# Second block: softplus attention in head pairs, two units ahead, and 256-column products split into high and low parts

## The chip, the cores and the metric

The kernel runs on one core of a Trainium2 chip. The metric is the device time of one execution in microseconds (us). Three runs of the kernel before gave 3783.95, 3784.22 and 3786.22 us, so the median is 3784.22 us. One more execution was profiled. TensorE is called PE below, VectorE DVE, ScalarE ACT, GpSimd POOL and SyncE SP.

## What is computed

Two transformer trunks of depth 2 follow one another, on 256 tokens of width 1024. All arithmetic is in fp32. The first block (gated linear attention, latent attention, a convolution module and a convolutional feed-forward, with 256 context tokens beside the 256 tokens in its first layer) is not touched. The second block, with what matters of its reference:

```python
h = x
for i in range(2):
    u = rms_norm(h, g_mix_pre[i])
    y = stick_breaking_attention(...) if i == 0 else dilated_attention(...)
    h = h + rms_norm(y, g_mix_post[i])
    u = rms_norm(h, g_ffn_pre[i])
    f = square(relu(u @ w_ff_in[i])) @ w_ff_out[i]      # 1024 -> 4096 -> 1024
    h = h + rms_norm(f, g_ffn_post[i])
    gate = sigmoid(rms_norm(h, g_ple[i]) @ w_ple_gate[i])
    h = h + (p[i] @ w_ple[i]) * gate

# stick breaking, 16 heads of 64, per head:
z = q @ k.T / 8
log_fail = where(past, log_sigmoid(-z), 0)              # -softplus(z)
later = reverse_cumsum(log_fail) - log_fail
a = where(past, exp(log_sigmoid(z) + later), 0);  out = a @ v
# dilated: 3 groups (dilation 1, 4, 16) of 8 heads of 64, rotary on q and k,
# softmax per group, groups joined by their log-sum-exp; in the kernel one
# softmax over the 3 x 256 masked scores of a head and a query
```

The projections are `x @ w_in_sb` (1024 x 3072) and `x @ w_in_dil` (1024 x 4608).

## The kernel before

There is no scheduler. Each engine's program is written out by hand, as one function per engine, and a `Plan` object gives every PSUM tile (a result of up to 128 x 512 in one of eight banks) its place in PE's order, its bank and its semaphore count. The activations lie transposed: 8 tiles `k` of 128 features by 256 tokens.

**Weights.** SP streams them through `wring`, a ring of three slots of 1 MB. A chunk is 8 x 128 input rows by 256 output columns (or 16 x 128 rows by 128 columns for `w_ff_out`). The load of chunk n waits until PE is through with chunk n - 3 (line 621 and the lines around it).

**Products.** `cols` (L712) makes one output tile of 128 features by 256 tokens with 8 fp32 matmuls, the weights as the stationary operand. `rows_of` (L734) does the same for values, with the activations stationary and 256 columns of weights moving. `deep` (L752) sums over 32 input tiles for `w_ff_out`. The profile shows each fp32 matmul as two records, each with its own weight load.

In the second block there are 128 such products of 256 columns in `sqk` (queries and keys of layer 0), 64 in `sv` (its values), 192 in `dqk`, 96 in `dv` (layer 1), 256 in each layer's `ffin`, 256 in each `ffout` and 64 in each `pg` (the gate): 1632 in all. `b2out` (the attention's output projection) and `pw` are such products too.

**Split products.** The first block's layer 0 feed-forward already makes its products another way: ACT copies a weight tile as `fp32r` into `weights_hi`, POOL subtracts to give `weights_lo`, the activations are split likewise, and `parts` (L687) makes high x high, high x low and low x high, three `fp32r` matmuls per input tile, 512 columns each.

**Norms.** `sums` (L786) adds 8 tiles of squares. DVE's `rms` (L1787, L1780, L1782) and ACT's `root` give 1/rms. `pre` (L2197) then writes the operand, 8 multiplies of 128 x 256, and `post` (L2204, L2206) adds the normed result to the residual.

**Stick-breaking attention.** Head by head. PE: `logits` one head ahead (L1111, L1112), cumulative sums against a triangle of ones (L1124 to L1127), then for each second head the values of two heads (L1136 to L1138). ACT: scaled copy of z, Abs, Exp, Ln, and later Exp of the argument; a table load stands between Ln and Exp. DVE: `failures` (L2243, L2244), `argument` (L2253, L2255), the mask (L2260) and the output copy (L2266).

**Dilated attention.** 16 units (8 head slots x 2 query tiles; an even unit has 3 blocks of keys, an odd one 6). PE: scores (L1160) one unit ahead, transposes of the probabilities (L793), then the values (L1179), which wait for ACT's copy of the transposes. DVE: mask and maximum (L2289, L2293), the probabilities (L2310), the output copy (L2301).

**Feed-forward.** `ffin`: PE makes 32 tiles; ACT takes Relu out of PSUM (L1235) and DVE squares (L2318). `ffout` follows when all of `ff_h` is there.

Of the kernel before, what the change touches and what calls it, by code (L numbers as in the profile page):

```python
# [56 lines left out]
def shape_constants():  # L57
# [39 lines left out]
    strict = i[:, None] < i[None, :]  # L97
    add("stick", np.concatenate([strict, np.ones((P, P)), strict], 1), 1)
# [40 lines left out]
class Plan:  # L139
# [3 lines left out]
    def __init__(self):  # L143
# [6 lines left out]
        self.units, self.unit_at, self.split_after = [], {}, {}  # L150

# [24 lines left out]
    def gemm(self, name, chunks, split=lambda i: False, after=lambda: None):  # L176
# [4 lines left out]
        for i, (loads, ends) in enumerate(chunks):  # L181
# [22 lines left out]
def build(nc, a, consts, late_consts, masks, const_at, out):  # L204
# [68 lines left out]
    HF, _ = area(s_at, ("ff_h", [P, FT2, SEQ]))  # L273
# [3 lines left out]
    PD, PDT, _ = area(t_at, ("dil_probs", [P, 1, 768]), ("dil_probs_t", [P, 1, 768]))  # L277
# [181 lines left out]
    for l in range(2):  # L459
        pl.tiles(f"mpre{l}", 1)  # L460
        if l == 0:
            cols_phase("sqk", W["w_in_sb_2"][0], 0, 2 * D, False)
            value_phase("sv", W["w_in_sb_2"][0], range(2 * D, 3 * D, 256), 1, False)
            pl.tiles("sz0", 1)
            for h in range(16):
                if h < 15:
                    pl.tiles(f"sz{h + 1}", 1)
                pl.tiles(f"sc{h}", 1)
                if h % 2:
                    pl.tiles(f"so{h // 2}", 1)  # L470
            cols_phase("b2out0", W["w_out_sb_2"][0], 0, D, False)
        else:
            wd = W["w_in_dil_2"][0]
            pl.gemm("dqk", [(cols_chunk(wd, g * 1536 + c), 2) for g in range(3) for c in range(0, 1024, 256)])
            pl.tiles("drot", 24)
            value_phase("dv", wd, [g * 1536 + 1024 + c for g in range(3) for c in (0, 256)], 1, False)
            units("d", 16, lambda u: u % 2 + 1, lambda u: u % 2 + 1)
# [3 lines left out]
        cols_phase(f"ffin{l}", W["w_ff_in_2"][l], 0, FF2, False)  # L481
        deep_phase(f"ffout{l}", W["w_ff_out_2"][l], 16)
# [5 lines left out]
        cols_phase(f"pg{l}", W["w_ple_gate_2"][l], 0, D, False)  # L488
# [29 lines left out]
    def bank(t, n0=0, n1=512):  # L518
        return PS[:, pl.tile_bank[t], n0:n1]

# [141 lines left out]
    def _(pe):  # L662
# [435 lines left out]
        for l in range(2):  # L1098
            sums(F[f"mpre{l}"], SQ2, 0, KD, SEQ, counter("squares", KD))
            if l == 0:  # L1100
# [15 lines left out]
                for h in range(16):  # L1116
                    if h < 15:
                        logits(h + 1)
# [114 lines left out]
    def _(act):  # L1233
# [374 lines left out]
        for l in range(2):  # L1608
# [40 lines left out]
            else:  # L1649
# [24 lines left out]
                for u in range(16):  # L1674
# [6 lines left out]
                    if u < 15:  # L1681
                        dexp(u + 1)
# [676 lines left out]
```

## Time and profile before

| | |
|---|---|
| median of 3 runs | 3784.22 us |
| the profiled execution | 3782.29 us |
| its span, first to last instruction | 3780.5 us |
| PE busy | 3365.9 us, 89% |
| weight loads (PEld) busy | 2397.9 us, 63% |
| DVE busy | 1420.6 us, 38% |
| ACT busy | 853.3 us, 23% |
| POOL busy | 150.8 us, 4% |
| mean granted PE clock | 0.93 |
| read from HBM | 358.70 MB, 95 GB/s |

The span is counted from the first to the last instruction; 1.8 us of the profiled execution lie outside of it. Busy times of an engine are those of its instructions, overlaps counted once. The granted clock is the share of 2.4 GHz that PE was given: 1.0 is 2.4 GHz and 0.5 is 1.2 GHz, and there are only these two levels. A group's mean ns is from issue to end, so that of a matmul (379 to 411 ns) is longer than the distance of two matmuls in a row; distances are read from a stretch's length and its count.

### The profile page before, as it was taken

To read this page: it belongs to the slowest core of one execution; us is meant where nothing else is said; L and a number is where in the kernel's file an instruction comes from. 1 tells how busy PE (TensorE), PEld (TensorE's weight loads), DVE (VectorE), ACT (ScalarE), POOL (GpSimd) and SP (SyncE) were. 2 spreads that over 40 slices of the span, in tenths; PEclk is the share of its full clock that TensorE was granted. 3 is DMA by queue.
4 is the path that set the end of the run, shared out by engine and by line. 5 is a ranking of instruction groups with operands and counts; after the bars stand their busy time and mean duration, and the time that the engine had idled before them with its cause. 6 is when DMAs were issued, how large, how long until landed. Compare 5 with 4: busy or idle time off the path is not lost.

```text
span 3780.5 us, 34902 instructions
## 1 busy us (share of the span) xinstructions
PE 3365.9 (89%) x14299; PEld 2397.9 (63%) x14299; DVE 1420.6 (38%) x2517; ACT 853.3 (23%) x1476; POOL 150.8 (4%) x125
## 2 busy tenths in 40 slices
PE   6987898999999699989888999898868998977998
PEld 3655544444444588436776678787757887755887
DVE  2267785232211588123579321542032102223102
ACT  4033210132221333013320332211262102112101
POOL 4000000000000244000000000000000000000000
PEclk9988899999999899999989999998958999966999
DMA  5212134323333132222223323344402553301453
GB/s 190 72 51 56 34 112 135 90 68 112 101 104 108 57 100 90 69 65 78 57 66 110 94 83 129 123 142 128 133 1 87 149 154 111 112 28 42 135 155 100
DMA packets 419421, 362.00 MB, mean 96 GB/s; under 512 B 20848, under 2 KB 392612, under 8 KB 419264
## 3 DMA queue, kind: packets, MB, share of 16 engines
q1 hardware_dynamic: 416928, 359.11, 30.8%
q8 instruction: 114, 1.87, 0.2%
q0 software_dynamic: 2336, 0.67, 0.1%
q14 instruction: 43, 0.35, 0.0%
HBM read 358.70 MB, written 1.05 MB: 95 GB/s over the span
## 4 chain that ended last, share of the span: by engine, by line
PE 77%; DVE 14%; ACT 4%; issue 2%; DMA 1%; POOL 1%; DVEq 0%; ACTq 0%; POOLq 0%
PE banks L712 24%; PE banks L770 12%; PE banks L752 12%; PE banks L687 6%; PE banks L734 5%; DVE conv_out L1954 4%; PE banks L786 3%; ACT L1235 2%; PE banks L1014 2%; PE banks L793 1%; PE banks L1005 1%; DVE gla_att L2016 1%; POOL vector_rows L650 1%; PE banks L955 1%; PE banks L938 1%
## 5 line engine op out<-in xcount | busy, mean ns | idle before, releaser
L712 PE MATMUL banks<-operand_a,wring 128*128 128x256 f32 (+1 forms) x3104 | 769.5, 411 | 44.2 <-DVE operand_a L1750 29.1
L712 PEld LDWEIGHTS banks<-operand_a,wring 128*128 128x128 f32 x3104 | 599.2, 193 | 214.0 <-issue 138.2
L1954 DVE SCALAR_TENSOR_TENSOR conv_out<-conv_in,vectors,conv_out 128x512 f32<-128x512 f32 (+1 forms) x464 | 286.8, 618 | 15.2
L770 PE MATMUL banks<-operand_a,wring 128*128 128x512 f32 (+1 forms) x768 | 263.9, 499 | 21.9 <-DMA wring<-in_w_in_dram 12.8
L770 PEld LDWEIGHTS banks<-operand_a,wring 128*128 128x128 f32 x768 | 146.0, 194 | 132.0 <-issue 98.0
L752 PE MATMUL banks<-ffn_h,wring 128*128 128x512 f32 (+1 forms) x704 | 227.4, 486 | 0.0
L752 PE MATMUL banks<-ff_h,wring 128*128 128x256 f32 x1024 | 221.3, 379 | 0.0
L752 PEld LDWEIGHTS banks<-ff_h,wring 128*128 128x128 f32 x1024 | 194.6, 190 | 26.5
L1005 PE MATMUL banks<-operand_a,wring 128*128 128x512 f32 (+1 forms) x512 | 182.9, 514 | 19.4 <-DVE conv_in L1972 19.4
L752 PEld LDWEIGHTS banks<-ffn_h,wring 128*128 128x128 f32 x704 | 133.8, 190 | 92.9 <-issue 83.5
L770 PE MATMUL banks<-operand_b,wring 128*128 128x512 f32 (+1 forms) x512 | 174.0, 497 | 17.0 <-DMA wring<-in_mla_wo_dram 6.0
L734 PE MATMUL banks<-wring,operand_a 128*128 128x256 f32 x832 | 180.3, 379 | 0.5 <-DVE tmp_dve L1837 0.5
L1235 ACT ACT_TABLE_LOAD x137 | 175.8, 1283 | 3.1 <-PEq L2347 0.7
L734 PEld LDWEIGHTS banks<-wring,operand_a 128*128 128x128 f32 x832 | 158.0, 190 | 22.8 <-issue 1.4
L687 PE MATMUL banks<-operand_a_hi,weights_hi 128*128 128x512 f32 x352 | 138.0, 392 | 29.9 <-POOL weights_lo L655 29.9
L655 POOL TENSOR_TENSOR weights_lo<-wring,weights_hi 128x1024 fp32r<-128x1024 f32 x44 | 108.9, 2476 | 1356.3 <-ACT weights_hi L1235 1356.3
L1005 PEld LDWEIGHTS banks<-operand_a,wring 128*128 128x128 f32 x512 | 102.4, 205 | 84.6 <-issue 76.6
L770 PEld LDWEIGHTS banks<-operand_b,wring 128*128 128x128 f32 x512 | 97.2, 193 | 84.6 <-issue 65.6
L687 PE MATMUL banks<-operand_a_lo,weights_hi 128*128 128x512 f32 x352 | 137.7, 391 | 0.0
L687 PE MATMUL banks<-operand_a_hi,weights_lo 128*128 128x512 f32 x352 | 137.7, 391 | 0.0
L1825 DVE SCALAR_TENSOR_TENSOR resid<-resid,tmp_act 128x512 f32<-128x512 f32 (+1 forms) x32 | 17.9, 559 | 283.1 <-ACT tmp_act L1315 283.1
L1787 DVE TENSOR_SCALAR gate_rank<-banks 128x256 f32<-128x256 f32 x10 | 4.2, 425 | 295.2 <-PE banks L786 295.2
(302 smaller groups left out, 4088.1 us busy)
## 6 DMA issues: line engine op xcount, KB each, us to landing
wring<-in_w_in_dram SPq DMA_DIRECT2D x52, 1024.0 KB, 5.3
wring<-in_w_ada_dram SPq DMA_DIRECT2D x48, 1024.0 KB, 6.5
wring<-in_ffn_wup_dram SPq DMA_DIRECT2D x44, 1024.0 KB, 5.1
wring<-in_w_ff_in_dram SPq DMA_DIRECT2D x32, 1024.0 KB, 5.5
wring<-in_w_ff_out_dram SPq DMA_DIRECT2D x32, 1024.0 KB, 5.6
wring<-in_ffn_wdown_dram SPq DMA_DIRECT2D x32, 704.0 KB, 4.5
wring<-in_w_in_dram SPq DMA_DIRECT2D x36, 512.0 KB, 5.2
wring<-in_w_in_dil_dram SPq DMA_DIRECT2D x18, 1024.0 KB, 5.0
```

The source lines that it names most:

```text
L650: pool.dma_start(VS[r % P:r % P + k, r // P, rep * w:rep * w + w], SRC[name][did:did + k, :]).then_inc(ev("rows_in"), 16)
L655: pool.tensor_tensor(WL[:, u % 2, :, :], w, WH[:, u % 2, :, :].bitcast(F32), ALU.subtract).then_inc(ev("w_lo"), 1)
L687: mm = pe.matmul(bank(t, 0, n), w[:, k, :], x[:, k, 0:n], start=first, stop=last)
L712: mm = pe.matmul(bank(t, 0, n), w[:, k, j * P:(j + 1) * P], opnd[:, k, 0:n], start=k == 0, stop=k == kt - 1)
L734: mm = pe.matmul(bank(t, j * 256, j * 256 + 256), AF[:, k, tok * P:(tok + 1) * P], w[:, k, :], start=k == 0, stop=k == KD - 1)
L752: mm = pe.matmul(bank(t, 0, n), w[:, k % per, :], opnd[:, k, 0:n], start=k == 0, stop=k == kt - 1)
L770: mm = pe.matmul(bank(t + j, 0, n), w[:, k, j * P:(j + 1) * P], (AF if gate else opnd)[:, k, 0:n], start=k == 0, stop=k == KD - 1)
L786: mm = pe.matmul(bank(t, 0, n), cn("ones"), src[:, m, 0:n], start=m == m0, stop=m == m1 - 1)
L1005: mm = pe.matmul(bank(t, 0, n), w[:, k, :], AF[:, k, 0:n], start=k == 0, stop=k == KD - 1)
L1014: mm = pe.matmul(bank(t + j, 0, n), w[:, k, j * P:(j + 1) * P], AF[:, k, 0:n], start=k == 0, stop=k == KD - 1)
L1235: act.activation(dst, src, f, **kw).then_inc(*inc)
L1954: own(stt(dst, src, w, dst, ALU.mult, ALU.add))
```

## The change

It touches the second block alone.

1. **Narrow products.** `narrow_gemm`, `narrow_cols`, `narrow_rows` and `narrow_deep` replace `cols_a`, `rows_of` and `deep` in `sqk`, `sv`, `dqk`, `dv`, `ffin`, `ffout` and `pg`. For each half chunk (8 tiles of 128 x 128 weights, a "unit") ACT makes `narrow_hi` (a copy as `fp32r`) and DVE `narrow_lo` (the difference). There are four buffers of each, filled up to three units ahead of PE's tile. `thrice` issues three `fp32r` matmuls of 256 columns for each input tile. A ring slot is freed when `narrow_lo` has been made of it.
2. **Operands.** `pre` makes the activations in full, ACT copies them as high parts (`narrow_operand`), and DVE subtracts for the low ones, tile by tile.
3. **Feed-forward in two halves.** `ffin` makes 16 tiles, `ffout` sums over them, then both again; ACT keeps the first half's sum in `b2_y` and DVE adds the second. Relu and square are now both DVE's (L2556, L2558), then ACT's high copy and DVE's low difference (L2544).
4. **Stick-breaking attention.** Two heads (one pair) per step, 768 columns per instruction. DVE scales z and adds a mask of 0 and -1e30, ACT applies `Softplus` to it, and the products with a mask go. Logits are made two pairs ahead.
5. **Dilated attention.** Scores two units ahead, two buffers of probabilities and of their transposes, values one unit behind. The rotations (`drot`) run inside `dqk`.

The core of it, in this order: the three matmuls, ACT's high parts, DVE's low parts, `ffin` on ACT, `ffin` on DVE, DVE's `pre`, ACT in the stick-breaking attention and PE in the dilated one.

```diff
+        def thrice(out, v, k, a, first, last):
+            wh, wl = NH[:, v % 4, k, :], NL[:, v % 4, k, :]
+            pe.matmul(out, wh, a[:, 0:SEQ], start=first, stop=False)
+            pe.matmul(out, wh, a[:, SEQ:512], start=False, stop=False)
+            return pe.matmul(out, wl, a[:, 0:SEQ], start=False, stop=last)
...
+        def narrow(u, more=3):
+            while n_narrow[0] <= u + more and narrow_near(n_narrow[0], u):
+                v = n_narrow[0]
+                n_narrow[0] += 1
+                c, w = narrow_weights(v)
+                act.wait_ge(ring_in[c % RING], ring_count[c])
+                if v >= 4:
+                    act.wait_ge(pe_done["gemm"], pl.narrow_done[v - 4])
+                op(NH[:, v % 4, :, :], w, ACT.Copy, (ev("narrow_hi"), 1))
...
+                dve.wait_ge(ev("narrow_hi"), v + 1)
+                tt(NL[:, v % 4, :, :], w, NH[:, v % 4, :, :].bitcast(F32), ALU.subtract).then_inc(ev("narrow_lo"), 1)
...
+                for m in range(16):
+                    narrow(pl.narrow_first[f"ffin{l}.{h}"] + m)
+                    act.wait_ge(ev("ff_full"), FT2 * l + 16 * h + m + 1)
...
+                    op(HN[:, m, 0:SEQ], TD[:, 2 + m % 2, 0:SEQ], ACT.Copy, (ev("ff_hi"), 1))
...
+                for m in range(16):
+                    t = F[f"ffin{l}.{h}"] + m
+                    x = TD[:, 2 + m % 2, 0:SEQ]
+                    narrow(pl.narrow_first[f"ffin{l}.{h}"] + m)
+                    if m:
+                        low_half(m - 1)
+                    dve.wait_ge(*done(t))
+                    if m >= 2:
+                        dve.wait_ge(ev("ff_h"), FT2 * l + 16 * h + m - 1)
+                    ts(x, bank(t, 0, SEQ), 0.0, None, ALU.max).then_inc(*free(t))
+                    dve.wait_ge(*freed(t))
+                    tt(x, x, x, ALU.mult).then_inc(ev("ff_full"), 1)
...
+            for m in range(KD + 1):
+                if m < KD:
+                    stt(TD[:, m % 2, 0:SEQ], X[:, m, 0:SEQ], vec(g, m), RS, ALU.mult, ALU.mult)\
+                        .then_inc(ev("n_full"), 1)
+                if m:
+                    n_low[0] += 1
+                    dve.wait_ge(ev("n_hi"), n_low[0])
+                    tt(AN[:, m - 1, SEQ:512], TD[:, (m - 1) % 2, 0:SEQ], AN[:, m - 1, 0:SEQ].bitcast(F32),
+                       ALU.subtract).then_inc(ev("operand_a"), 1)
...
+                for p in range(8):
+                    if p + 1 < 8:
+                        softplus(p + 1)
+                    act.wait_ge(ev("stick_arg"), p + 1)
+                    x = XS[:, p % 2, :, :]
+                    op(x, x, ACT.Exp, (ev("stick_exp"), 1))
...
+                for u in range(17):
+                    if u < 16:
+                        counter("probs", 1)(0)
+                        for jt in range(u % 2 + 1):
+                            turn(F[f"d.t{u}"] + jt,
+                                 [PD[:, u % 2, jt * 384 + g * P:jt * 384 + (g + 1) * P] for g in range(3)])
+                    if u:
+                        dvalues(u - 1)
+                    if u + 2 < 16:
+                        dscores(u + 2)
```

How the instructions now stand at three places. First DVE in the feed-forward of layer 0. Before, after the 8 multiplies of the operand (L2197), one square per tile:

```order
L2197 SCALAR_TENSOR_TENSOR operand_a<-resid,vectors,gate_rank 128x256 [waits pe_done,dve_chain]
L2197 SCALAR_TENSOR_TENSOR operand_a<-resid,vectors,gate_rank 128x256 x7
L2318 TENSOR_TENSOR ff_h<-ff_h 128x256 [waits bank_free4]
L2318 TENSOR_TENSOR ff_h<-ff_h 128x256 [waits bank_free5]
L2318 TENSOR_TENSOR ff_h<-ff_h 128x256 [waits bank_free6]
```

After, from the last low part of the operand (L2405) on:

```order
L2405 TENSOR_TENSOR operand_narrow<-tmp_dve,operand_narrow 128x256 [waits n_hi,operand_a]
L2393 TENSOR_TENSOR narrow_lo<-wring,narrow_hi 128x1024 [waits narrow_hi,operand_a]
L2393 TENSOR_TENSOR narrow_lo<-wring,narrow_hi 128x1024 [waits narrow_hi]
L2556 TENSOR_SCALAR tmp_dve<-banks 128x256 [waits pe_done]
L2558 TENSOR_TENSOR tmp_dve<-tmp_dve 128x256 [waits bank_free0]
L2393 TENSOR_TENSOR narrow_lo<-wring,narrow_hi 128x1024 [waits narrow_hi]
L2544 TENSOR_TENSOR ff_h<-tmp_dve,ff_h 128x256 [waits ff_hi]
L2556 TENSOR_SCALAR tmp_dve<-banks 128x256 [waits pe_done]
L2558 TENSOR_TENSOR tmp_dve<-tmp_dve 128x256 [waits bank_free1]
```

DVE has four instructions per tile where it had one, and the first of them waits for ACT's next high part.

Second, ACT at the same place. Before, it was one row of 32 Relu copies; now high copies of the hidden tile and of the weights take turns:

```order
L1378 ACTIVATE ff_h<-tmp_dve 128x256 [waits ff_full]
L1378 ACTIVATE narrow_hi<-wring 128x1024 [waits pe_done,ring_in2]
L1378 ACTIVATE ff_h<-tmp_dve 128x256 [waits ff_full]
L1378 ACTIVATE narrow_hi<-wring 128x1024 [waits pe_done,ring_in2]
L1378 ACTIVATE ff_h<-tmp_dve 128x256 [waits ff_full]
```

Each weight copy stands behind the copy of a hidden tile, which waits for DVE's square of that tile (`ff_full`).

Third, PE in the dilated attention (L1160 scores, L793 transposes, L1179 values). Before:

```order
L793 MATMUL banks<-consts,dil_probs 128x128 [waits bank_free1,probs]
L793 MATMUL banks<-consts,dil_probs 128x128 x2
L1179 MATMUL banks<-dil_probs_t,b_v 64x128 [waits bank_free2,bank_free1]
L1179 MATMUL banks<-dil_probs_t,b_v 64x128 x2
L1160 MATMUL banks<-b_qk 128x128 [waits bank_free3]
L1160 MATMUL banks<-b_qk 128x128 x2
```

After (L1295 scores, L916 transposes, L1308 values), an odd unit's transposes first:

```order
L916 MATMUL banks<-consts,dil_probs 128x128 [waits bank_free5,probs]
L916 MATMUL banks<-consts,dil_probs 128x128 x2
L916 MATMUL banks<-consts,dil_probs 128x128 [waits bank_free6]
L916 MATMUL banks<-consts,dil_probs 128x128 x2
L1308 MATMUL banks<-dil_probs_t,b_v 64x128 [waits bank_free7,bank_free3]
L1308 MATMUL banks<-dil_probs_t,b_v 64x128 x2
L1295 MATMUL banks<-b_qk 128x128 [waits bank_free0]
L1295 MATMUL banks<-b_qk 128x128 x2
```

The values are now those of the unit before, and the scores those of two units later. They still stand behind the transposes, which wait for `probs`.

## Rows read from the trace of the kernel before

**Rows 1.** The page, part 1: busy time of each engine, its share, its instructions.

```profile
PE 3365.9 (89%) x14299; PEld 2397.9 (63%) x14299; DVE 1420.6 (38%) x2517; ACT 853.3 (23%) x1476; POOL 150.8 (4%) x125
```

**Rows 2.** Stages: stretch, length, busy PE, PEld, DVE, ACT, POOL, clock, DMA share, GB/s.

```profile
2725.00:2847.00 122.00, 71.47 (x289) 58.71 (x289) 44.36 (x87) 83.14 (x114) 0.00 (x0) 0.52 0.03 9
3327.00:3461.00 134.00, 87.75 (x362) 71.59 (x360) 40.96 (x104) 25.81 (x58) 0.00 (x0) 0.51 0.01 4
1880.00:1900.00 20.00, 12.90 (x66) 11.40 (x67) 14.52 (x28) 8.41 (x9) 0.00 (x0) 0.91 0.21 53
1900.00:1920.00 20.00, 15.50 (x72) 13.29 (x71) 16.59 (x31) 5.29 (x6) 0.00 (x0) 0.77 0.21 54
```

**Rows 3.** The chain that ended last, second block: start, length, what.

```profile
2638.85 58.31 PE banks L712 x256
2697.16 27.64 PE banks L734 x128
...
2895.29 113.35 PE banks L712 x512
3008.64 110.51 PE banks L752 x512
...
3143.70 27.64 PE banks L712 x128
...
3179.66 84.82 PE banks L712 x384
3285.61 41.69 PE banks L734 x192
...
3497.66 112.43 PE banks L712 x512
```

**Rows 4.** The same chain in the first block: split products, and 128-column fp32 matmuls.

```profile
1271.47 241.71 PE banks L687 x1056
...
1842.44 1.80 PE banks L889 x16
```

**Rows 5.** The tile weights_hi: ACT's high copies, ns min/median/max, first and last start.

```profile
L1235 ACT ACTIVATE weights_hi<-wring x44: 1040/1052/1055, 1267.9 to 1503.0; 128x1024 fp32r<-128x1024 f32 x44
```

**Rows 6.** Groups by form, 2600 to 3780 us: DVE and ACT instructions.

```profile
L1235 ACT ACT_TABLE_LOAD x38 | 48.8, 1283 | 0.7
L2318 DVE TENSOR_TENSOR ff_h<-ff_h 128x256 f32<-128x256 f32 x64 | 27.2, 425 | 195.1 <-ACT ff_h L1235 195.1
L1235 ACT ACTIVATE b_sq<-resid 128x256 f32<-128x256 f32 x48 | 18.4, 411 | 27.0 <-DVE resid L2206 27.0
L2244 DVE TENSOR_TENSOR tmp_dve<-tmp_dve,late_consts 128x384 f32<-128x384 f32 x16 | 8.9, 558 | 0.6
L1235 ACT ACTIVATE dil_probs<-tmp_dve,stats 128x768 f32<-128x768 f32 x8 | 7.4, 926 | 0.0
```

**Rows 7.** PE in the dilated attention, half clock, in order of time.

```profile
3391.21 1.54 PE banks L793 x6
3393.38 2.79 PE banks L1179 x12
3396.17 2.87 PE banks L1160 x12
...
3401.45 0.92 PE banks L793 x3
3402.93 1.54 PE banks L1179 x6
3404.47 1.59 PE banks L1160 x6
```

**Rows 8.** In order of time, 3118 to 3150 us: start, length, engine, line, what.

```profile
3126.18 0.42 DVE L2206 TENSOR_TENSOR resid<-resid,tmp_dve 128x256 f32<-128x256 f32 x1
3126.64 0.42 ACT L1235 ACTIVATE b_sq<-resid 128x256 f32<-128x256 f32 x1 [2.80 <-DVE resid L2206]
...
3137.80 3.26 DVE L2197 SCALAR_TENSOR_TENSOR operand_a<-resid,vectors,gate_rank 128x256 f32<-128x256 f32 x8
```

More of the change, by code:

```diff
@@ L198, in gemm, with narrow_gemm @@
                 self.chunk_at[c] = self.signals["gemm"]
+    def narrow_gemm(self, name, chunks, tiles_of):
+        self.narrow_first[name] = len(self.narrow)
+        self.reserve(name, sum(sum(ends) for _, ends in chunks))
+        self.chunk0[name], t = len(self.chunk_at), self.first[name]
+        for loads, ends in chunks:
+            c = len(self.loads)
+            self.loads.append(loads)
+            for j in range(2):
+                self.narrow.append((c, j))
+            if tiles_of == "rows":
+                self.place(t)
+                t += 1
+                self.narrow_done += 2 * [self.signals["gemm"]]
+            else:
+                for j in range(2):
+                    if ends[j]:
+                        self.place(t)
+                        t += 1
+                    else:
+                        self.signals["gemm"] += 1
+                    self.narrow_done.append(self.signals["gemm"])
+            self.chunk_at.append(self.signals["gemm"])
+            self.narrow_after[c] = len(self.narrow)
     def last(self, name):
@@ L630, in _, with narrow_weights, narrow_near @@
         sp.wait_ge(ev("stored"), 32)
+    def narrow_weights(v):
+        c, j = pl.narrow[v]
+        _, kt, n = pl.loads[c][0][0]
+        w = part(c, (0, kt, n))
+        return c, w[:, :, j * P:(j + 1) * P] if kt == KD else w[:, j * KD:(j + 1) * KD, :]
+    def narrow_near(v, u):
+        return v < len(pl.narrow) and pl.narrow[v][0] < pl.narrow[u][0] + RING
     def unit(u):
@@ new lines, in narrow_deep @@
+        def narrow_deep(name, half, ready):
+            for m in range(KD):
+                t = F[f"{name}.{half}"] + m
+                start_tile(t)
+                out = bank(t, 0, SEQ)
+                for j in range(2):
+                    v = pl.narrow_first[f"{name}.{half}"] + 2 * m + j
+                    pe.wait_ge(ev("narrow_lo"), v + 1)
+                    for k in range(KD):
+                        if m == 0:
+                            ready(KD * j + k)
+                        mm = thrice(out, v, k, HN[:, KD * j + k, :], j + k == 0, j == 1 and k == KD - 1)
+                    mm.then_inc(*made(t))
@@ L1115, in _ @@
[L1115 to L1135 removed]
+                    z = banks(t, 384)
@@ L1188, in _ @@
             sums(F[f"fpre{l}"], SQ2, 0, KD, SEQ, counter("squares", KD))
-            cols_a(f"ffin{l}", SEQ, a_ready())
-            deep(f"ffout{l}", FT2, 16, HF, SEQ, counter("ff_h", FT2))
+            ready = a_ready()
+            for h in range(2):
+                run(narrow_cols(f"ffin{l}.{h}", None if h else ready))
+                narrow_deep(f"ffout{l}", h, counter("ff_h", 16))
             sums(F[f"fpost{l}"], SQ2, 0, KD, SEQ, counter("squares", KD))
@@ L2276, in _, with rotated @@
+                logits(0)
+                for p in range(8):
+                    if p + 1 < 8:
+                        logits(p + 1)
+                    argument(p)
+                    if p:
+                        outputs(p - 1)
+                outputs(7)
+            else:
+                def rotated(i):
+                    rotate(F["drot"] + i, QK[:, i, :], CS[:, :], SN[:, :], "rope_d", i % 2)
                 for i in range(24):
-                    dve.wait_ge(*freed(F["dqk"] + i))
```

414 lines of the change are left out of this document (263 added, 151 removed).

## The prediction

> **What bounds the kernel now.** I read the page's busy times first: PE is busy for 89% of the span, every other engine for 38% or less [rows 1]. So PE, or what PE waits for, sets the time. The chain of waits then gives the second block as a list of stages. The products stand there one after another, each stage as long as its matmuls: ffin 113.35 and 112.43 us, ffout 110.51 in either layer, sqk 58.31, sv 27.64, dqk 84.82, dv 41.69, pg 27.64 twice [rows 3]. Together these are 714 us for 1632 products, 0.437 us each; a pure run is ffout's 110.51 us for 256, **0.432 us a product, 3.46 us a tile of 8**. Between them lie two stages that the products don't fill: the stick-breaking attention (from 2724.8 to 2847.0 us) and the dilated one (3327.3 to 3461.5). By stages, PE is busy there for only 71 of 122 and 88 of 134 us, at a granted clock of 0.52 and 0.51 [rows 2]: PE waits for a chain over ACT and DVE, and what it does itself runs at 1.2 GHz. In the first of them ACT is busy for 83 us. DMA takes a small share in both.
>
> **The price of a narrow product.** The first block's split products make 1056 fp32r matmuls of 512 columns in 241.71 us, 0.229 us each, at full clock [rows 4]. No row has one of 256 columns. From below it costs 256/2.4 GHz = 0.107 us; from above 0.229, if not the columns but the weight load sets the distance. A row near it: 16 records of 128-column fp32 matmuls, each with a weight load of its own, came in 1.80 us, 0.1125 us each [rows 4]. So a load of 128 columns fits under 0.11 us. I take **0.111 us, 24 of them a tile of 2.66 us** in place of 3.46.
>
> The Trainium skill (TensorE: Matmul & The Clock Gate, "Measured speedup vs the span model") says that a weight load overlaps running matmuls only where their row groups differ. Each matmul here uses all row groups, so by it load and matmul would add up, and by its load time of 107 ns (same page, "LDWEIGHTS (loading the stationary operand)") a tile would be an estimated 5.1 us and the change a large loss. The rows just named speak against it.
>
> **The change part by part.** All against the profiled execution, 3782.3 us.
>
> *sqk, sv, dv.* ACT makes a high part in 1.05 us [rows 5] and a copy in about 0.4; DVE's subtraction of 1024 columns has no row. 256 columns take 0.425 us and 384 take 0.558 [rows 6], 1.04 ns a column, so 1.22 us; bounds are ACT's 1.05 and four times 0.425, 1.70. Both engines stay under 2.66, and there are four buffers, so PE sets the pace. sqk: 16 x 2.66 = 42.6, plus the 3.0 us by which 58.3 exceeds 16 x 3.46, plus the operand. In `pre`, DVE wrote the 8 operand tiles in 3.26 us [rows 8], one per 0.41. Now multiply, ACT's copy and subtraction alternate: 0.41 + 0.42 + 0.04 = 0.87 us per tile, with 0.04 us from one engine's end to the next one's start [rows 8]. The first output tile thus ends about 4.7 us later. 50.3 for 58.3: **-8**. sv: 4 x 5.33 for 27.6: **-6**. dv: 6 x 5.33 for 41.7: **-10**.
>
> *dqk and the rotations.* These took 3179.7 to 3285.6 us, 105.9 with the rotations behind [rows 3]. Each tile is now 2.66 + 0.44 for a rotation; DVE has 1.2 + three of 0.42, which hides. 24 x 3.1 + 4.7 + 1.9 = 81: **-25**.
>
> *pg.* 6.4 gained on the tiles, 5.1 lost on the operand, whose copies stand behind the pw evacuations on ACT: **-3** for both.
>
> *Feed-forward.* ffout is PE-bound, 2.66 a tile. In ffin there is a **new loop**: DVE's square of tile m (0.425) lets ACT copy the hidden tile, behind which stands the high part of the weights of tile m+4. DVE's low part waits for that, and behind it stand low half, Relu and square of tile m+1. Added up with the handoffs, and with 0.07 to 0.1 us of overlap where two in a row are independent: 0.04 + 0.31 + 1.05 + 0.04 + 1.15 + 0.36 + 0.42 + 0.04 + 0.43 = **3.85 us a tile**, more than PE's 2.66 and more than the 3.46 of before. PE starts with four tiles in hand, which are used up after some four tiles. At each half's end PE waits for the last low half before ffout's first tile can finish. I count 63 us from the first high part to the end of ffout's second unit, then 14 x 2.66 = 37: 100 us for a second half, 108 for a first one with its operand. 2 x 208 = 415 for 447: **-32**. The longer subtraction (1.70) would take it to about zero.
>
> *Stick-breaking attention.* Per pair PE has two logits of 256 and two of 128 columns, 8 sums, 6 value products: 4.5 us at full clock, 8.9 at half. ACT has two table loads of 1.283 and two passes over 768 columns, 0.926 each as Exp shows [rows 6]: 4.4. DVE has 2.9. With logits two pairs ahead no longer chain remains. 8 x 4.5 + 10 for filling and emptying = 46, for 122: **-76**. Bounds: 42, and 80 at half clock. PE would be busy nearly throughout, so I take the full clock.
>
> *Dilated attention.* Scores of unit u+2 stand behind the transposes of unit u, which wait for `probs`; DVE needs these scores before it makes the next `probs`. So "two ahead" doesn't open the loop; only ACT's copy leaves it. That was the gap from the transposes' end to the values' start, 0.63 us for an odd unit (3392.75 to 3393.38) and 0.56 for an even one [rows 7]: 8 pairs x 1.19 = **-10**. At full clock PE's 11.3 us of the 16.8 that a pair takes (134.2/8) would halve, 45 us more. I take half, as now [rows 2].
>
> *Rest.* The second half's sum goes over DVE before ACT squares it: +1. The loads stay covered: 1 MB now serves 5.3 us instead of 6.9.
>
> **Sum:** -8 - 6 - 10 - 25 - 3 - 32 - 76 - 10 + 1 = -169. ffin leaves PE idle for 1.2 us in each 3.85. In the first block, with PE busy for 12.9 and 15.5 of 20 us, the clock was 0.91 and 0.77 [rows 2]; I add 8 us for some of that. 3782.3 - 161 = 3621 for an execution like the profiled one; the median of the runs lies 1.9 us above it, so **3623 us**.
>
> **Rivals.**
> - *A, the forecast*, 3585 to 3660 (subtraction and matmul a little off): 0.57.
> - *B, the clock falls in the new gaps.* With ffin at 1.2 GHz, 24 matmuls take 5.3 us, 1.45 above the loop: 64 tiles, +93; the stick attention at half clock, +34. 3621 - 8 + 127 = 3740; half of it gives 3680. For it: the first block's clock at such shares. Against: those gaps were longer ones, and at half clock PE is never idle. 0.19. The Trainium skill (same page, "A second HAM failure mode: psum-queue depth-cycling") tells of a kernel whose many small idles between groups made the clock go back and forth; no row here has gaps of this size and spacing.
> - *C, the dilated attention gets the full clock*, and matmuls cost 0.107: 45 and 13 us off, 3565. For it: PE's work is in one piece now. Against: its busy share rises only from 66% to about 71% (88 of 124 us). 0.19.
> - *D, slower: the weight load sets the distance of an fp32r matmul.* At 0.229 a tile is 5.5 us: 204 tiles x 2.03 = +414, rotations -10, operands +25, attentions -86: 4125. It decides from about 0.16 us a matmul on (3360 PE-bound matmuls x 0.048 = 161). The 0.1125 of [rows 4] speaks against it. 0.03.
> - *E, the reordering gains nothing in the attentions and the subtraction costs 1.70*: 3782 - 161 + 32 + 86 = 3739, still faster: 0.02.
>
> **Numbers.** The forecast is A's. The range, 3545 to 3705, leaves out B's far half, D and a part of C. A measurement of this kernel can tell 0.2%, some 7.6 us, from no change: only D ends above, and a mixture of B and E could reach the band. Faster 0.95, same 0.01, slower 0.04.
>
> **What would show it.** In the profile after: fp32r matmuls 0.11 us apart in ffout, whose last 14 units of a half take 37 us; low parts at 1.2 us; in ffin one low part per 3.85 us and PE idle on `narrow_lo`; the stick attention at 46 us and a clock near 1.0; the dilated one at 124 us and 0.5. A matmul distance over 0.16, or a clock near 0.5 in the feed-forward, would make it wrong.

## The result and the profile after

| | before | after |
|---|---|---|
| median of the runs, same chip | 3785.22 us (3783.95 to 3787.65) | **3616.27 us** (3615.60 to 3616.82) |
| the profiled execution | 3782.3 | 3616.7 |
| its span | 3780.5 | 3614.6 |

The median before is now that of four runs. The ratio is **0.9553, 95% interval 0.9536 to 0.9569**: faster by 4.5%. The forecast was 3623 us, range 3545 to 3705. The total came out 7 us off, and three of its terms by 8 to 15 us each: what follows is mostly about those.

The page after, part 1, busy time of each engine as in [rows 1]:

```profile
PE 3214.1 (89%) x15931; PEld 2335.8 (65%) x15931; DVE 1715.0 (47%) x2857; ACT 1024.0 (28%) x1645; POOL 150.9 (4%) x125
```

PE's share stays at 89%: its work fell by 152 us, about as much as the span. DVE carries 294 us more and ACT 171.

The stages of the second block, in the order stick attention, dilated attention, then ffin, ffout, ffin, ffout of layer 0, dqk with the rotations, dv, sqk, sv. The columns are those of [rows 2]:

```profile
2717.80:2755.80 38.00, 31.83 (x290) 27.91 (x289) 21.91 (x31) 32.06 (x31) 0.00 (x0) 1.00 0.00 1
3195.70:3304.80 109.10, 72.25 (x361) 60.07 (x361) 41.23 (x104) 27.39 (x58) 0.00 (x0) 0.72 0.00 1
2803.80:2860.60 56.80, 52.59 (x384) 50.25 (x384) 36.83 (x66) 22.15 (x34) 0.00 (x0) 0.92 0.41 121
2861.30:2913.20 51.90, 48.42 (x386) 47.85 (x387) 25.54 (x28) 21.68 (x28) 0.00 (x0) 0.97 0.63 179
2913.10:2964.50 51.40, 47.70 (x386) 46.30 (x384) 30.52 (x52) 19.09 (x28) 0.00 (x0) 1.00 0.48 144
2965.20:3015.70 50.50, 47.06 (x385) 46.48 (x386) 26.62 (x34) 20.98 (x27) 0.00 (x0) 1.00 0.59 173
3077.30:3159.80 82.50, 82.49 (x619) 80.56 (x620) 57.56 (x100) 36.07 (x56) 0.00 (x0) 0.95 0.46 152
3160.80:3195.70 34.90, 34.88 (x290) 34.65 (x288) 13.46 (x17) 10.97 (x14) 0.00 (x0) 1.00 0.33 106
2645.30:2694.60 49.30, 48.86 (x384) 47.70 (x385) 24.84 (x29) 23.42 (x37) 0.00 (x0) 0.97 0.50 160
2694.60:2717.80 23.20, 23.20 (x194) 23.03 (x192) 9.67 (x16) 6.91 (x9) 0.00 (x0) 1.00 0.49 160
```

What to see: the clock is 0.92 or more in all these stretches except in the dilated attention; PE is busy without a break in dqk, sv and dv, and is not in ffin and ffout, although ffout has no loop of its own. The stage lengths give the account (us; before from [rows 2, 3] and the same stretches of that trace):

| stage | before | after | change | forecast |
|---|---|---|---|---|
| sqk | 58.3 | 49.5 | -8.8 | -8 |
| sv | 27.6 | 23.2 | -4.4 | -6 |
| dqk, rotations | 105.9 | 83.5 | -22.4 | -25 |
| dv | 41.7 | 34.9 | -6.8 | -10 |
| two feed-forwards | 446.8 | 426.4 | -20.4 | -32 |
| stick attention | 122.2 | 38.0 | -84.2 | -76 |
| dilated attention | 134.2 | 109.1 | -25.1 | -10 |
| pg, both | 55.3 | 56.6 | +1.3 | -3 |
| b2out, both | 45.9 | 41.9 | -4.0 | 0 |
| start of the second block | 2638.85 | 2645.30 | +6.5 | 0 |
| the rest | | | +2.4 | +9 |
| sum | | | -165.9 | -161 |

The price of a narrow matmul, PE in order of time in sv (start, length, line, tiles):

```profile
2700.03 0.28 PE L843 MATMUL banks<-narrow_hi,operand_narrow 128*128 128x256 f32 x1
2700.15 0.28 PE L844 MATMUL banks<-narrow_lo,operand_narrow 128*128 128x256 f32 x1
```

The starts are **0.120 us** apart (the lengths overlap; the next ones start at 2700.27 and 2700.39), so 24 matmuls take 2.88 us. The forecast said 0.111 and 2.66. Each of these matmuls has a weight load of its own with all rows. The distance holds 256 columns at 2.4 GHz (0.1067 us) and 0.0133 us more, and no load beside them. By the rule of the Trainium skill that the prediction weighed, a load overlaps running matmuls only where the row groups differ (TensorE: Matmul & The Clock Gate, "The mechanism", at its end, just ahead of the section that the prediction named); this row disagrees.

The loop in ffin, on DVE in order of time (in brackets the idle time before, and what ended it):

```profile
2926.03 1.23 DVE L2393 TENSOR_TENSOR narrow_lo<-wring,narrow_hi 128x1024 fp32r<-128x1024 f32 x1 [1.43 <-ACT narrow_hi L1378]
2927.17 0.42 DVE L2544 TENSOR_TENSOR ff_h<-tmp_dve,ff_h 128x256 fp32r<-128x256 f32 x1
2927.51 0.42 DVE L2556 TENSOR_SCALAR tmp_dve<-banks 128x256 f32<-128x256 f32 x1
2927.96 0.42 DVE L2558 TENSOR_TENSOR tmp_dve<-tmp_dve 128x256 f32<-128x256 f32 x1
2929.82 1.23 DVE L2393 TENSOR_TENSOR narrow_lo<-wring,narrow_hi 128x1024 fp32r<-128x1024 f32 x1 [1.43 <-ACT narrow_hi L1378]
```

and on ACT:

```profile
2928.42 0.42 ACT L1378 ACTIVATE ff_h<-tmp_dve 128x256 fp32r<-128x256 f32 x1 [2.42 <-DVE tmp_dve L2558]
2928.74 1.04 ACT L1378 ACTIVATE narrow_hi<-wring 128x1024 fp32r<-128x1024 f32 x1
```

One low part per **3.79 us**, DVE waiting 1.43 us in each for ACT's high part, ACT waiting 2.42 us for DVE's square. Neither engine is busy all the time, each stands behind the other. PE, at 2.88 us a tile, lives at first on the tiles in hand and then feels it. The second half, PE alone in order of time (a wait like the first comes every 3.79 us):

```profile
2946.24 0.38 PE L814 MATMUL banks<-operand_narrow,narrow_hi 128*128 128x256 f32 x1 [0.65 <-DVE narrow_lo L2393]
...
2973.08 0.39 PE L814 MATMUL banks<-ff_h,narrow_hi 128*128 128x256 f32 x1 [1.70 <-DVE ff_h L2544]
...
2974.78 0.39 PE L814 MATMUL banks<-ff_h,narrow_hi 128*128 128x256 f32 x1 [1.08 <-DVE ff_h L2544]
```

The wait runs over into ffout: its first tiles wait for the last low parts and then for the last low half of `ff_h`. The clock stayed at 1.00 through these gaps (a window in the midst of them, columns as above):

```profile
2943.50:2951.10 7.60, 6.30 (x51) 5.89 (x50) 4.67 (x9) 2.73 (x4) 0.00 (x0) 1.00 0.50 138
```

That is not so at every end of ffin. The two waits for `ff_h`, 1.7 and 1.1 us, come in all four halves, and right behind them the clock fell to half in three: for 3.2 us in the first half of either layer, and for 5.8 us in the second half of layer 1. In the second half of layer 0, with the same two waits, it did not. The fall in layer 0, and that in the second half of layer 1 with the matmul that begins it:

```profile
2870.90:2874.10 3.20, 3.20 (x15) 3.20 (x16) 2.73 (x3) 2.60 (x4) 0.00 (x0) 0.51 0.10 30
3510.00:3515.80 5.80, 5.75 (x27) 5.75 (x28) 3.83 (x4) 2.79 (x4) 0.00 (x0) 0.50 0.50 147
3510.05 0.58 PE L814 MATMUL banks<-ff_h,narrow_hi 128*128 128x256 f32 x1 [1.08 <-DVE ff_h L2544]
```

A matmul takes 0.213 us there in place of 0.120, so these 15, 15 and 27 matmuls cost 5.3 us in all.

The stick attention, ACT in order of time:

```profile
2734.86 1.28 ACT L1378 ACT_TABLE_LOAD   x1
2736.15 0.84 ACT L1378 ACTIVATE stick_failures<-stick_z 128x768 f32<-128x768 f32 x1
2737.01 1.28 ACT L1378 ACT_TABLE_LOAD   x1
2738.31 0.84 ACT L1378 ACTIVATE stick_arg<-stick_arg 128x768 f32<-128x768 f32 x1
2739.17 1.28 ACT L1378 ACT_TABLE_LOAD   x1
```

ACT has no gap: 4.31 us a pair (2734.86 to 2739.17), 2.57 of them table loads. ACT is the bound here, as PE is elsewhere. The dilated attention, PE in order of time:

```profile
3266.16 1.79 PE L1295 MATMUL banks<-b_qk 64*128 64x128 f32 x12
3270.38 0.90 PE L916 MATMUL banks<-consts,dil_probs 128*128 128x128 f32 x3 [2.42 <-DVE dil_probs L2531]
3271.21 2.58 PE L1308 MATMUL banks<-dil_probs_t,b_v 128*64 128x128 f32 x12
3273.72 0.93 PE L1295 MATMUL banks<-b_qk 64*128 64x128 f32 x6
3276.88 1.54 PE L916 MATMUL banks<-consts,dil_probs 128*128 128x128 f32 x6 [2.22 <-DVE dil_probs L2531]
```

PE idles 2.2 to 2.4 us before each set of transposes. The scores are at full clock or near it (12 in 1.79, 6 in 0.93 us; 2.87 and 1.59 in [rows 7]), the transposes and the values mostly at half (6 transposes in 1.54, as in [rows 7]): the clock changes back and forth within a pair, and the mean granted is 0.72.

### The profile page after: what moved, and what is told of

It reads as the page before. It is cut to its first block, busy times and chain, and to the rows that moved or that the text cites. A ratio compares the mean times of both kernels' runs of the same rounds, so it can differ in the third digit from the quotient of the medians.

```text
span 3614.6 us, 38987 instructions
## 1 busy us (share of the span) xinstructions
PE 3214.1 (89%) x15931; PEld 2335.8 (65%) x15931; DVE 1715.0 (47%) x2857; ACT 1024.0 (28%) x1645; POOL 150.9 (4%) x125
## 4 chain that ended last, share of the span: by engine, by line
PE 73%; DVE 17%; issue 4%; ACT 4%; DMA 1%; POOL 1%; DVEq 0%; ACTq 0%; POOLq 0%
PE banks L783 13%; PE banks L893 13%; PE banks L758 7%; PE banks L875 6%; DVE conv_out L2145 5%; PE banks L814 4%; PE banks L815 4%; PE banks L816 4%; PE banks L805 3%; PE banks L909 3%; PE banks L1137 2%; ACT narrow_hi L1378 2%; PE banks L916 1%; PE banks L1128 1%; DVE gla_att L2207 1%
## 5 line engine op out<-in xcount | busy, mean ns | idle before, releaser
L2393 DVE TENSOR_TENSOR narrow_lo<-wring,narrow_hi 128x1024 fp32r<-128x1024 f32 x204 | 248.0, 1224 | 266.4 <-ACT narrow_hi L1378 265.8
L783 PE MATMUL banks<-operand_a,wring 128*128 128x256 f32 (+1 forms) x1184 | 345.4, 455 | 29.1 <-DVE operand_a L1941 29.1
L814 PE MATMUL banks<-operand_narrow,narrow_hi 128*128 128x256 f32 x960 | 289.4, 301 | 41.1 <-DVE operand_narrow L2405 24.3
L783 PEld LDWEIGHTS banks<-operand_a,wring 128*128 128x128 f32 x1184 | 228.8, 194 | 145.5 <-issue 121.3
L815 PE MATMUL banks<-operand_narrow,narrow_hi 128*128 128x256 f32 x960 | 276.4, 288 | 0.0
L816 PE MATMUL banks<-operand_narrow,narrow_lo 128*128 128x256 f32 x960 | 276.2, 288 | 0.0
L893 PEld LDWEIGHTS banks<-operand_a,wring 128*128 128x128 f32 x768 | 146.0, 194 | 132.9 <-issue 98.1
L1378 ACT ACTIVATE narrow_hi<-wring 128x1024 fp32r<-128x1024 f32 x204 | 212.0, 1049 | 67.6 <-PE banks L816 66.2
L814 PEld LDWEIGHTS banks<-operand_narrow,narrow_hi 128*128 128x128 f32 x960 | 187.9, 196 | 55.6 <-issue 23.5
L875 PEld LDWEIGHTS banks<-ffn_h,wring 128*128 128x128 f32 x704 | 133.8, 190 | 92.9 <-issue 83.5
L815 PEld LDWEIGHTS banks<-operand_narrow,narrow_hi 128*128 128x128 f32 x960 | 189.4, 197 | 0.6
L816 PEld LDWEIGHTS banks<-operand_narrow,narrow_lo 128*128 128x128 f32 x960 | 189.0, 197 | 0.0
L814 PE MATMUL banks<-ff_h,narrow_hi 128*128 128x256 f32 x512 | 149.1, 291 | 16.5 <-DVE ff_h L2544 11.2
L1128 PEld LDWEIGHTS banks<-operand_a,wring 128*128 128x128 f32 x512 | 102.6, 206 | 84.7 <-issue 76.8
```

The costliest lines, as they stand in the source:

```text
L783: mm = pe.matmul(bank(t, 0, n), w[:, k, j * P:(j + 1) * P], opnd[:, k, 0:n], start=k == 0, stop=k == kt - 1)
L814: pe.matmul(out, wh, a[:, 0:SEQ], start=first, stop=False)
L815: pe.matmul(out, wh, a[:, SEQ:512], start=False, stop=False)
L816: return pe.matmul(out, wl, a[:, 0:SEQ], start=False, stop=last)
L875: mm = pe.matmul(bank(t, 0, n), w[:, k % per, :], opnd[:, k, 0:n], start=k == 0, stop=k == kt - 1)
L893: mm = pe.matmul(bank(t + j, 0, n), w[:, k, j * P:(j + 1) * P], (AF if gate else opnd)[:, k, 0:n], start=k == 0, stop=k == KD - 1)
```

## The experiments

Two theories stood after this. **The loop theory:** the two remaining losses are orders of the program, not amounts of work: in ffin, ACT and DVE wait for one another in a ring; in the dilated attention, the scores that DVE wants stand behind transposes that wait for DVE. **The load theory:** PE, DVE and ACT simply have that much to do (DVE's low parts, the dilated softmax), or PE pays for the clock. The first four kernels ran on one chip beside the kernel before (3786.19 us, 3780.93 to 3791.06), the other four likewise (3785.07, 3783.16 to 3789.28). All edits but that of f4 are made on the changed kernel.

### f1: Relu and square ahead of low part and low half

```diff
                     x = TD[:, 2 + m % 2, 0:SEQ]
-                    narrow(pl.narrow_first[f"ffin{l}.{h}"] + m)
-                    if m:
-                        low_half(m - 1)
+                    if m == 0:
+                        narrow(pl.narrow_first[f"ffin{l}.{h}"])
                     dve.wait_ge(*done(t))
 ...
                     tt(x, x, x, ALU.mult).then_inc(ev("ff_full"), 1)
+                    if m:
+                        low_half(m - 1)
+                        narrow(pl.narrow_first[f"ffin{l}.{h}"] + m)
                 low_half(15)
```

> The changed kernel, with DVE's order in ffin alone changed: Relu and square of tile m first, then the low half of tile m-1, then the low part of the weights. Theory: the 3.79 us per tile seen in ffin after the change is a loop (square, ACT's hidden copy, ACT's high part, DVE's low part, low half, Relu, square). With the low part behind the square the loop is open, DVE's 2.4 us and ACT's 1.4 us hide under PE's 2.88 us, and each layer's feed-forward takes about 189 us instead of 212 and 214: 46 us less than the changed kernel, near 3570 us. Rival: ffin is bound by what DVE and ACT have to do in sum, not by its order; then it stays near 3616 us.

Measured: 3566.49 us (3564.95 to 3567.22), ratio 0.9419 (0.9405 to 0.9433), 50 us below the changed kernel. The windows of the second half, ffin and ffout:

```profile
2897.30:2943.40 46.10, 46.10 (x387) 46.10 (x386) 34.59 (x59) 21.86 (x32) 0.00 (x0) 1.00 0.57 170
2943.40:2989.40 46.00, 46.00 (x385) 46.00 (x385) 23.30 (x27) 18.49 (x23) 0.00 (x0) 1.00 0.62 183
```

and DVE in order of time:

```profile
2920.51 0.42 DVE L2555 TENSOR_SCALAR tmp_dve<-banks 128x256 f32<-128x256 f32 x1 [0.52 <-PE banks L816]
...
2921.31 0.42 DVE L2544 TENSOR_TENSOR ff_h<-tmp_dve,ff_h 128x256 fp32r<-128x256 f32 x1
2921.65 1.22 DVE L2393 TENSOR_TENSOR narrow_lo<-wring,narrow_hi 128x1024 fp32r<-128x1024 f32 x1
2923.39 0.42 DVE L2555 TENSOR_SCALAR tmp_dve<-banks 128x256 f32<-128x256 f32 x1 [0.52 <-PE banks L816]
```

The same four instructions per tile now take 2.88 us, DVE waits for PE and not for ACT, and PE is busy in every bit of both stages: 16 x 2.88 = 46.1. The waits at ffout's start have gone too, and with them every fall of the clock at the ends of ffin: of the 50 us some 5 are the clock's. DVE's load was never the bound; the loop theory holds for ffin.

### f2: scores of unit u+2 ahead of the transposes of unit u

```diff
                 for u in range(17):
+                    if u + 2 < 16:
+                        dscores(u + 2)
                     if u < 16:
 ...
                         dvalues(u - 1)
-                    if u + 2 < 16:
-                        dscores(u + 2)
```

with the same move in the plan of the tiles.

> The changed kernel, with PE's order in the dilated attention alone changed: the scores of unit u+2 before the transposes of unit u. Theory: the stage is bound by the loop probs, transposes, values, scores, maximum, probs; with the scores ahead of the wait, one turn of the loop serves two units, DVE's work (some 6 us a pair) becomes the bound at full clock, and the stage falls from 109 to about 55 us: near 3562 us. If PE stays at half clock it needs 11.3 us a pair, 93 us, 3600 us. Rival: the stage hangs on DVE's and ACT's latencies for each unit whatever PE's order is; then nothing changes, 3616 us.

Measured: 3559.43 us (3552.92 to 3561.59), ratio 0.9398 (0.9382 to 0.9414), 57 us below the changed kernel. The dilated attention as a window, and PE in order of time:

```profile
3195.40:3250.30 54.90, 50.09 (x361) 42.14 (x360) 41.22 (x104) 26.55 (x58) 0.00 (x0) 0.94 0.00 1
```

```profile
3222.78 1.60 PE L1295 MATMUL banks<-b_qk 64*128 64x128 f32 x12
3224.31 0.88 PE L916 MATMUL banks<-consts,dil_probs 128*128 128x128 f32 x6
3225.12 0.87 PE L1308 MATMUL banks<-dil_probs_t,b_v 128*64 128x128 f32 x6
3225.92 0.93 PE L1295 MATMUL banks<-b_qk 64*128 64x128 f32 x6
```

The stage is half as long, 54.9 for 109.1 us, with equal instructions. The waits of 2.2 and 2.4 us are gone, a pair takes 5.96 us, and the clock is 0.94: 6 transposes take 0.88 us where they took 1.54. The order alone opened the loop, and the clock followed. How the gain divides between the two isn't told apart, as no run has the one without the other. Outside of the stage, layer 1's fall of the clock behind ffin is missing in this trace, 2.5 of the 57 us.

### f3: both moves

> Both orders together. If the two losses are independent, their gains add: about 3516 us. If one feeds on the other (the clock, the ring), less.

Measured: **3515.16 us** (3513.74 to 3517.76), ratio 0.9285 (0.9271 to 0.9299). This version beats both kernels: 101 us below the changed one, where the two gains add up to 107. Of the missing 5.5 us, 2.5 are layer 1's fall of the clock, which is absent in f1 and in f2 and so counted twice; the others are not traced here. Its page:

```profile
span 3511.9 us, 38987 instructions
...
PE 3179.8 (91%) x15931; PEld 2315.7 (66%) x15931; DVE 1715.9 (49%) x2857; ACT 1023.8 (29%) x1645; POOL 151.0 (4%) x125
```

The number of instructions is that of the changed kernel; only their order differs.

### f4: the attentions alone

The kernel before, with only the changed code of the two attentions.

> The kernel before, with only the two attention stages of the change (pairs, Softplus, two units ahead, double buffers); all products stay fp32. Theory: the stages take what they take in the changed kernel, 38 us instead of 122 and 109 instead of 134, and the projection behind each gains 1 and 3 us: 3785 - 113 = 3672 us. The rest of the change, some 56 us, is then the split products. Rival: part of the attention's gain comes from the products around it (clock, weights already there); then it stays above 3690 us.

Measured: 3672.27 us (3670.81 to 3672.80), ratio 0.9699 (0.9684 to 0.9713). The stick attention took 37.9 us at a clock of 1.00, as in the changed kernel. The dilated attention as a window:

```profile
3245.00:3354.80 109.80, 72.97 (x360) 60.46 (x360) 41.23 (x104) 27.41 (x58) 0.00 (x0) 0.69 0.02 5
```

So the attentions bring 113 us by themselves, and the rest of the change, the split products with their feed-forward in halves, the other 56 (3672.27 - 3616.27). The dilated stage is the same with products that aren't split: its shortening belongs to its own code.

### g5: logits one pair ahead, not two

```diff
                 logits(0)
-                logits(1)
                 for p in range(9):
+                    if p + 1 < 8:
+                        logits(p + 1)
 ...
-                    if p + 2 < 8:
-                        logits(p + 2)
```

> The changed kernel, with the logits of the stick-breaking attention one pair ahead instead of two (the dilated attention as changed). Theory: ACT bounds a pair at 4.31 us (two table loads and two passes, without a gap in the trace after the change), and with one pair ahead the mask is ready before ACT asks for it, so nothing changes: 3616 us, stage 38 us. The stage's gain is then that of pairs and Softplus. Rival: the second pair ahead opened the chain; then a pair takes at least logits, mask and Softplus more, some 3 us, 24 us in all: 3640 us.

Measured: 3615.47 us (3613.28 to 3618.02), ratio 0.9551 (0.9535 to 0.9567): no difference to the changed kernel. The stage took 37.9 us again, ACT busy for 32.05 of them.

The second unit ahead is worth nothing here, because the first one, issued ahead of the sums, already keeps ACT fed. What is left as the reason for the shorter stage is ACT's work, 83.1 us before [rows 2] and 32.1 after, now two passes a pair with two table loads. Pairs, Softplus and the dropped products with the mask aren't told apart: no run has one without the others.

### g6: Softplus twice

```diff
+                    own(LF[:, p % 2, :, :], ZS[:, p % 2, :, :], ACT.Softplus)
                     op(LF[:, p % 2, :, :], ZS[:, p % 2, :, :], ACT.Softplus, (ev("failures"), 1))
```

> The changed kernel, with every Softplus of 768 columns done twice in a row (same input, same output). ACT-bound theory: 8 x 0.86 us more, 3623 us, stage 45 us. Rival, PE-bound (a pair's matmuls were put at 4.5 us in the prediction, against ACT's 4.4): less than half of that.

Measured: 3621.34 us (3620.58 to 3622.09), ratio 0.9567 (0.9548 to 0.9586). The stage as a window:

```profile
2715.00:2760.30 45.30, 34.80 (x290) 30.36 (x289) 22.11 (x31) 38.68 (x39) 0.00 (x0) 0.92 0.00 1
```

It grew by 7.3 us for 8 more passes of 0.84, 6.7 us of work that all lands in the stage: ACT sets it. The median rose by only 5. In this execution the dilated attention, with equal instructions, took 104.1 us in place of 109.1, at a clock of 0.74:

```profile
3202.60:3306.70 104.10, 68.81 (x349) 57.11 (x350) 40.62 (x102) 26.62 (x57) 0.00 (x0) 0.74 0.00 1
```

So the length of that stage moves by 5 us between programs, and with it its mean clock; that where the clock changes fall makes the length is argued, not tested. A difference of that size in the total is no evidence on the stage that was edited.

### g7: four matmuls a product

```diff
             pe.matmul(out, wh, a[:, SEQ:512], start=False, stop=False)
+            pe.matmul(out, wl, a[:, SEQ:512], start=False, stop=False)
```

> The changed kernel, with a fourth fp32r matmul per input tile (low x low) in the units of narrow_cols and narrow_deep; it adds the product of the two low parts. Theory: where PE sets the pace (16 units of sqk, 24 of dqk, 16 of pg, 64 of ffout) a unit grows by 8 x 0.120 = 0.96 us, together 115 us; in ffin's 64 units the loop of 3.79 us hides all of it, since 32 x 0.120 = 3.84: near 3734 us. Rival: PE sets the pace in ffin too: 177 us more, 3793 us.

Measured: 3739.31 us (3738.45 to 3740.18), ratio 0.9879 (0.9859 to 0.9899), 123 us above the changed kernel: near the theory's 3734, far from the rival's 3793. The ffin of the second half as a window (the ffout ahead of it reads alike, 61.50 of 61.50):

```profile
2942.30:3003.70 61.40, 61.40 (x514) 61.40 (x514) 36.77 (x61) 21.81 (x32) 0.00 (x0) 1.00 0.46 134
```

A tile is 32 x 0.120 = 3.84 us, just above the loop's 3.79, and PE waits for nothing. A second half took 102.6 us (2913.1 to 3015.7); here 2 x 16 x 0.96 = 30.7 us were added to it, and it takes 122.9, only 20.3 more. The other 10.4 us are the waits that the added work filled, the same 10 that f1 takes out of a half (102.6 to 92.2). It is also a warning: with a third more matmuls PE shows 100% in ffin, and nothing in the busy times tells that a loop of 3.79 us stands just behind PE's 3.84.

### g8: high x both halves as one matmul of 512 columns

```diff
-            pe.matmul(out, wh, a[:, 0:SEQ], start=first, stop=False)
-            pe.matmul(out, wh, a[:, SEQ:512], start=False, stop=False)
-            return pe.matmul(out, wl, a[:, 0:SEQ], start=False, stop=last)
+            pe.matmul(out, wh, a[:, 0:512], start=first, stop=False)
+            return pe.matmul(out[:, 0:SEQ], wl, a[:, 0:SEQ], start=False, stop=last)
```

`out` is now the whole bank. The kernel leaves high x low out of its result.

> The changed kernel, with high x high and high x low as one fp32r matmul of 512 columns into a whole bank, and low x high into its first half as before. It leaves out the addition of the two halves, so high x low is missing from the output. Theory: an fp32r matmul costs its columns at 2.4 GHz plus 13.3 ns whatever its width (512 columns came at 0.2267 us, 256 at 0.120): 8 x 13.3 ns less in each of 120 PE-bound units, 13 us: 3603 us. Rival: the extra over 2.4 GHz goes with the columns (a rate, not a price per instruction): no change, 3616 us.

Measured: 3604.87 us (3601.50 to 3610.86), ratio 0.9525 (0.9511 to 0.9540). The runs lie 9 us apart, so the 11 us gained agree with the theory's 13 only roughly; the distances decide. PE in order of time in dqk:

```profile
3100.11 0.28 PE L815 MATMUL banks<-operand_narrow,narrow_lo 128*128 128x256 f32 x1
3100.22 0.39 PE L814 MATMUL banks<-operand_narrow,narrow_hi 128*128 128x512 f32 x1
3100.45 0.28 PE L815 MATMUL banks<-operand_narrow,narrow_lo 128*128 128x256 f32 x1
```

One matmul of each width takes 0.345 us (3100.11 to 3100.45 is 0.34), where three narrow ones take 0.360. Of 512 + 256 columns, 0.320 us, the rest is 0.025, nearly two times 0.0133; a price per column would give 0.360. The excess belongs to the matmul, not to the column. ffin, held by its loop, did not change (51.3 us).

## Why the prediction was right or wrong

The mechanism of case A came about, but for the clock: it changed back and forth in the dilated attention, and fell for short stretches in the feed-forward. That the total agrees to 7 us is luck, since errors of both signs cancelled.

**The narrow product: mis-sized.** The term "0.111 us, 24 of them a tile of 2.66 us" measured 0.120 and 2.88. I took the excess over pure columns from the 128-column fp32 row (0.1125). The row of the same type stood beside it: the 512-column fp32r matmuls of [rows 4] take 0.229, where the columns alone need 0.2133, and from start to start 0.2267. That excess, 0.0133 us, added to 256 columns gives 0.120 to the digit. It accounts for sv (-4.4 for -6), for most of dv (-6.8 for -10), for more than dqk's error (24 x 0.22 = 5.3, and -22.4 came for -25), and in the feed-forward for 2 x 14 x 0.22 = 6 us a layer. In sqk (-8.8 for -8) another error hid it: the 3.0 and 4.7 us that the prediction put on top of the 16 tiles came as 3.4 (49.5 - 16 x 2.88). The two pg got 1.3 us longer instead of 3 shorter: 16 x 0.22 = 3.5 are the price of the matmul, and 1.3 a fall of the clock in the second, from 3584.4 us on for 3.0 us.

**The feed-forward: right in its mechanism.** The loop was added up as 3.85 us and measured 3.79; the low part was taken as 1.22 us and is 1.224. "63 us to the end of ffout's second unit, then 37" came out as 62 and 41 (2913.1 to 2975, 2975 to 3015.7), and the first half as 109 for 108. The price of the matmul explains the 41 (14 x 2.88 = 40.3). Layer 0 took 211.9 us for the forecast 208. Layer 1 took 214.5: its 2.6 more are the fall of the clock from 3510.05 us on, 27 matmuls at 0.213 us, which layer 0 hasn't there. What the prediction did not draw from its own sum is that the loop is a matter of order alone: f1 takes out 50 us with the same instructions.

**The stick attention: sizes too large.** The step "8 x 4.5 + 10 = 46" took PE's 4.5 us and ACT's 4.4 and measured 38.0 us. Of the 8 us, 1.5 are the pair (8 x 4.5 against 8 x 4.31) and 6.5 the filling and emptying. ACT's pass over 768 columns takes 0.84 us and not the 0.926 of the row I used: that row was the dilated Exp, which also takes its bias from `stats` and sums its output, 0.94 us for 768 columns in the trace after, too. Which of the two costs the 0.1 us, no run shows. For PE I added up full prices, while matmuls of the two heads of a pair, on 64 rows each, overlap:

```profile
2740.34 0.71 PE L1236 MATMUL banks<-b_qk 64*128 64x256 f32 x4
2740.88 0.39 PE L1237 MATMUL banks<-b_qk 64*128 64x128 f32 x4
```

The four records of 256 columns take 0.54 us from the first start to the next group's, where four in a row took 0.86 in the products before (0.432 us for two). All 8 logit records are done 0.93 us after the first starts. PE is busy 31.8 of 38 us and not the bound; ACT is (g6). The 10 us for filling and emptying were 38.0 - 8 x 4.31 = 3.5. The full clock was rightly taken. That "logits two pairs ahead" leave no longer chain was true, but one ahead does as well (g5).

**The dilated attention: the clock was the wrong step.** "I take half, as now" gave 124 us; it was 109.1 at 0.72. The structure was as described: the 1.19 us of ACT's copy left the loop, as the values now start right at the transposes' end (3278.35, after 1.54 us from 3276.88 on). The order leaves the rest closed, and f2, which opens it, brings 54 us. The 15 us beyond the forecast are mostly the clock: from the third pair on the scores take 1.79 and 0.93 us for 2.87 and 1.59, 1.7 us a pair and some 10 in all. But a granted clock of 0.51 in a row before was carried over to a stage with a different pattern of work. Case C, the full clock, had 0.19; what came lies between the two. What makes the clock rise for the scores and fall for the transposes stays open here.

**Rivals.** B, the clock falls in ffin's gaps, came about only at three of the four ends of ffin, at a cost of 5.3 us in all; within ffin the clock stayed at 1.00 with PE short of work for 0.9 us of every 3.79 (3.79 - 2.88). The clock's going back and forth of the Trainium skill's "A second HAM failure mode: psum-queue depth-cycling" (TensorE: Matmul & The Clock Gate) is thus not seen in the gaps of 0.65 us within ffin, and is seen in the dilated attention, where the idle stretches are 2.2 to 2.4 us. D fell with the 0.120, as E did with the 1.224 of the subtraction. The 8 us added for the clock in ffin were of the right kind; 5.3 came, and they stand in the feed-forward's row of the table. In the row of the 8 us stands another loss: the second block starts 6.5 us later. Some 1 to 3 of them are ACT's three high parts (2.93 us) ahead of the squares and the operand's first low part. About 4 arise in the first block, most of it between 1071 and 1105 us, where the instructions are the same: from 1084 to 1105 us the clock is 0.92, and 1.00 in the kernel before. It is 1.00 there in f1 and f3 too, whose second blocks start at 2642.0 and 2641.8 us and not at 2645.3. So these 4 us vary between programs that are equal up to there; why stays open.

**What cancelled.** Too optimistic: sv, dv, dqk, pg and the feed-forward, 23 us together (1.6 + 3.2 + 2.6 + 4.3 + 11.6). Too pessimistic: the two attentions, 23 us (8.2 + 15.1), sqk, 0.8, and b2out behind the attentions, 4, since it no longer begins at the low clock (0.88 and 0.67 in its first 10 and 8 us before, 1.00 after).

## What to carry to other kernels

When work moves onto engines that serve one another in program order, add up the ring of waits as well as each engine's load. If the ring is longer, issue first the instruction that another engine waits for, and put work with slack (a weight tile four ahead) behind it: here two such moves were worth 101 us, more than the split products' 56. "n units ahead" helped here only where the early work was issued in front of the wait it is meant to cover (f2, g5). Price a new instruction by the row of the same type, as its columns plus that row's excess; and take a granted clock over from another stage as a range, never as a value.

## What was not expected of the hardware

- An fp32r matmul cost its columns at 2.4 GHz plus 0.0133 us, at 256 and at 512 columns alike (0.120 and 0.2267 from start to start; together 0.345 in g8), each with its own full weight load, which doesn't show.
- Matmuls of 64 rows for the two heads overlap: 8 records of logits in 0.93 us, and 4 of 256 columns in 0.54 for 0.86.
- The clock stayed at 1.00 with PE idle for 0.9 of every 3.79 us in ffin, fell for 3.2 to 5.8 us behind three of four pairs of waits of 1.7 and 1.1 us, and changed between its two levels within each 13.7 us pair of the dilated attention, where the idle stretches are 2.2 to 2.4 us. The same instructions there took 104.1 to 109.8 us in three kernels.
- Softplus and Exp alternating cost a table load of 1.28 us at each change, more than the pass over 768 columns itself (0.84).
